# A two-layer hybrid decoder trunk: compression layer 1 in four column groups with its weights beside the ring, and sparse scores over 128 rows

## The reference, cut to what matters

```
h = RMSNorm(x); proj = h @ W_in            (columns shared out among four mixers and their gates)
o_A = NSA(compressed + selected + sliding window)     4 heads of 64
o_B = S5 state-space scan + GLU
o_C = gated DeltaNet, chunks of 64
o_D = stick-breaking attention
x = x + W_out( sum_m sigmoid(g_m(h)) * (o_m @ P_m) )
x = x + SwiGLU(RMSNorm(x))                 (hidden width 2816)
```

## Time and profile before

| | |
|---|---|
| time, median of 3 runs | 2307.31 us (2302.64 to 2307.64) |
| the profiled execution, its own time | 2303.84 us |
| its span in the trace | 2302.1 us |
| mean granted TensorE clock in it, share of full | 0.959 |
| TensorE matmul busy | 2120.3 us, 92% |
| VectorE, ScalarE, GpSimd busy | 1144.4, 758.9, 538.6 us |
| weight slabs loaded | 296 of 512 KB |

### The profile page before, as it was taken

One profiled execution on the slowest core, in us unless ns is written; L12 is line 12 of the kernel. 1 busy time (PEld: TensorE's weight loads), 2 busy tenths in 40 slices (PEclk: granted clock), 3 DMA queues, 4 the chain that ended last, 5 costly groups with the idle time before them and its releaser, 6 DMA issues.

```text
span 2302.1 us, 25818 instructions
## 1 busy us (share of the span) xinstructions
PE 2120.3 (92%) x10100; PEld 1676.2 (73%) x10100; DVE 1144.4 (50%) x1575; ACT 758.9 (33%) x1149; POOL 538.6 (23%) x300
## 2 busy tenths in 40 slices
PE   5989998899999899999988889888999998999998
PEld 3667976667677688888756679766566776888886
DVE  6344569763347544432273365796533475444321
ACT  5333231264334322222152332313642343222221
POOL 2336027523116000000032350374131250000000
PEclk9999999999989999999989999999989899999999
DMA  4232011222124223333233310123121342332332
GB/s 144 101 104 80 15 46 60 83 69 69 55 102 166 80 92 100 94 100 101 67 99 101 117 49 15 51 69 97 55 69 42 126 153 69 100 101 92 101 101 92
DMA packets 55124, 197.03 MB, mean 86 GB/s; under 512 B 6112, under 2 KB 6112, under 8 KB 52576
## 3 DMA queue, kind: packets, MB, share of 16 engines
q1 hardware_dynamic: 43488, 161.85, 22.1%
q10 hardware_dynamic: 11520, 33.56, 3.8%
HBM read 176.51 MB, written 18.87 MB: 85 GB/s over the span
## 4 chain that ended last, share of the span: by engine, by line
PE 36%; DVE 8%; POOL 2%; ACT 2%; DMA 1%; issue 1%; SPq 0%; POOLq 0%; DVEq 0%; PEldq 0%; ACTq 0%
PE bank L455 9%; PE bank L457 9%; PE bank L456 9%; DVE arena L1636 2%; DVE arena L1631 1%; DMA raw<-weights 1%; PE bank L904 1%; PE bank L662 1%; PE bank L865 1%; PE bank L642 1%; POOL wL L1859 1%; PE bank L792 1%; DVE wL L1320 1%; DVE arena L1802 1%; ACT wH L1005 0%
## 5 line engine op out<-in xcount | busy, mean ns | idle before, releaser
L455 PE MATMUL bank<-hH,wH 128*128 128x512 f32 (+1 forms) x1536 | 620.7, 404 | 54.9 <-POOL wL L1859 27.4
L456 PE MATMUL bank<-hL,wH 128*128 128x512 f32 (+1 forms) x1536 | 609.9, 397 | 0.0
L457 PE MATMUL bank<-hH,wL 128*128 128x512 f32 (+1 forms) x1536 | 608.4, 396 | 0.0
L1859 POOL TENSOR_TENSOR wL<-raw,wH 128x1024 fp32r<-128x1024 f32 x114 | 281.6, 2474 | 1232.7 <-ACT wH L1005 1232.5
L1005 ACT ACTIVATE wH<-raw 128x1024 fp32r<-128x1024 f32 x276 | 290.2, 1053 | 395.9 <-PE bank L457 231.7
L455 PEld LDWEIGHTS bank<-hH,wH 128*128 128x128 f32 (+1 forms) x1536 | 294.9, 192 | 135.3 <-issue 36.4
L457 PEld LDWEIGHTS bank<-hH,wL 128*128 128x128 f32 (+1 forms) x1536 | 293.6, 191 | 65.6 <-issue 1.0
L456 PEld LDWEIGHTS bank<-hL,wH 128*128 128x128 f32 (+1 forms) x1536 | 294.4, 192 | 61.8 <-issue 1.0
L1320 DVE TENSOR_TENSOR wL<-raw,wH 128x1024 fp32r<-128x1024 f32 x162 | 213.3, 1317 | 185.3 <-ACT wH L1005 185.2
L1008 ACT ACTIVATE gst<-bank 128x512 f32<-128x512 f32 x64 | 38.2, 596 | 351.1 <-PE bank L457 351.1
L457 PE MATMUL bank<-hidH,wL 128*128 128x512 f32 x352 | 140.4, 399 | 0.0
(11 more groups left out here) (380 smaller groups left out, 3008.1 us busy)
## 6 DMA issues: line engine op xcount, KB each, us to landing
raw<-weights SPq DMA_DIRECT2D x296, 512.0 KB, 3.5
gates<-gst ACTq DMA_DIRECT2D x64, 256.0 KB, 2.4
gload<-gates ACTq DMA_DIRECT2D x16, 1024.0 KB, 6.9
xT<-x SPq DMA_DIRECT2D x1, 2048.0 KB, 10.1
out<-xT SPq DMA_DIRECT2D x1, 2048.0 KB, 6.7
const<-constants SPq DMA_DIRECT2D x1, 1228.5 KB, 5.5
pack<-params SPq DMA_DIRECT2D x2, 451.0 KB, 3.9
cosT<-pos SPq DMA_DIRECT2D x1, 256.0 KB, 5.6
```

The lines of the kernel that those rows point to most:

```text
L455: mm(out, a[0], b[0], start=start, stop=False)
L456: mm(out, a[0], b[1], start=False, stop=False)
L457: return mm(out, a[1], b[0], start=False, stop=stop)
L1859: tt_(wL[:, ORD[i] % SPLIT], raw[:, i % RING], wH[:, ORD[i] % SPLIT].bitcast(F32), SU)\
```

## The change

1. The eight slabs of w1 leave the ring: `RAW` keeps only cw2 and glu, and a layer streams 140 slabs in place of 148. They lie behind the stream in the same array. ScalarE's own queue loads them at the start of the layer, four (v) after the third slab is split and four (k) after h is complete, into memory that is idle then (`arena`, `pj`, `sbv`), each set with a semaphore. TensorE waits for each set once and no longer waits for its own matmuls or releases a buffer there.
2. The blocks are padded from 31 to 32 columns (GpSimd clears the 32nd), and the four matmuls of a step write to partitions 0, 32, 64 and 96 onwards of the bank, each group adding up over the four steps. The four partial sums are added where the result was transposed: a matmul with the constant `stack` (128 x 31, four stacked identities) takes the place of each transpose.
3. The sparse scores take all 128 rows: the weights are both heads' queries (`nqr[:, h // 2, ...]`), the keys are `kpad[h % 2]`, which holds them in the half of that head and zeros in the other. VectorE clears the two halves (two memsets of 64 x 1024 after the third `nts`), and TensorE waits for that too.
4. The mask after the weights of stick-breaking is made from `ge` in one scalar_tensor_tensor, in place of an addition of `negk`, which leaves the constants. `abc_done` and `trig_done` count what `tab_ready` and `sin_ready` did.

```diff
-RAW = [f"ck{i}" for i in range(4)] + [f"cv{i}" for i in range(4)] + ["cw2", "glu"]
+RAW = ["cw2", "glu"]
...
-        bk = comp[:, 2, 0:496].rearrange("p (b n) -> p b n", b=16)
-        bv = comp[:, 3, 0:496].rearrange("p (b n) -> p b n", b=16)
+        bk = comp[:, 2, :].rearrange("p (b n) -> p b n", b=16)
+        bv = comp[:, 3, :].rearrange("p (b n) -> p b n", b=16)
...
+        cmp_w = [[x.rearrange("p (c n) -> p c n", c=4) for x in xs] for xs in (
+            [arena[:, 4096 + 1024 * j:5120 + 1024 * j] for j in range(4)],
+            [pj[:, TI["sb0"] + 2 * j:TI["sb0"] + 2 * j + 2, :].rearrange("p a s -> p (a s)") for j in range(2)]
+            + [sbv[:, :, :].rearrange("p t c -> p (t c)"), arena[:, 11264:12288]])]
...
-        nqn, nqr, nsq, nrs, kdup = tiles(0, 3), tiles(1536, 3), tiles(3072, 3), tiles(4608, 3), tiles(6144, 2)
+        nqn, nqr, nsq, nrs = tiles(0, 3), tiles(1536, 3), tiles(3072, 3), tiles(4608, 3)
+        kpad = (tiles(6144, 2), pj[:, 4:6, :])
...
-                            name = f"c{'kv'[kv]}{j}"
-                            w = raw_slab(name).rearrange("p (k c) -> p k c", k=4)
-                            for i in range(4 * j, 4 * j + 4):
-                                last = mm(PS[6 + kv][0:NCMP, 0:256], blocks[:, i, :], w[:, i % 4, :],
-                                          start=(i == 0), stop=(i == 15))
-                            raw_used(last, name)
+                            if j == 0:
+                                pe.wait_ge(cmp_loaded[kv], 64)
+                            for c in range(4):
+                                last = mm(PS[6 + kv][32 * c:32 * c + 32, 0:256], blocks[:, 4 * j + c, :], cmp_w[kv][j][:, c, :],
+                                          start=(j == 0), stop=(j == 3))
+                        last.then_inc(q["cmp_nat"], 1)
...
-                        last = nc.tensor.transpose(PS[5][:, 31 * c:31 * c + 31], cmpT[0:NCMP, P * c:P * c + P],
-                                                   ident[0:NCMP, 0:NCMP])
+                        last = mm(PS[5][:, 31 * c:31 * c + 31], cmpT[:, P * c:P * c + P], cst("stack")[:, 0:NCMP],
+                                  start=True, stop=True)
...
-                    pe.wait_ge(q["t_sin"], 3)
+                    pe.wait_ge(q["t_sin"], 4)
...
-                            mm(out[:, 0:wid], nqr[half(h), h // 2, P * qt:P * qt + P], kdup[half(h), br, 0:wid],
+                            mm(out[:, 0:wid], nqr[:, h // 2, P * qt:P * qt + P], kpad[h % 2][:, br, 0:wid],
...
                     high_to(SPLIT)
+                    for j in range(4):
+                        a.dma_start(cmp_w[1][j], a_w[layer, NSLAB + 4 + j].rearrange("p (c n) -> p c n", c=4))\
+                            .then_inc(cmp_loaded[1], 16)
+                    a.wait_ge(q["h_ready"], KT)
+                    for j in range(4):
+                        a.dma_start(cmp_w[0][j], a_w[layer, NSLAB + j].rearrange("p (c n) -> p c n", c=4))\
+                            .then_inc(cmp_loaded[0], 16)
...
-                        a.wait_ge(q["slab_done"], SLAB[f"c{'kv'[kv]}3"] + 1)
-                        act(cmpT[0:NCMP, 256 * kv:256 * kv + 256], PS[6 + kv][0:NCMP, 0:256], ACT.Copy)\
+                        a.wait_ge(q["cmp_nat"], kv + 1)
+                        act(cmpT[:, 256 * kv:256 * kv + 256], PS[6 + kv][:, 0:256], ACT.Copy)\
                             .then_inc(q["cmp_nat_ready"], 1)
-                    high_to(ahead(SLAB["cv3"]))
                     fill(FILL["hidden"])
...
-                    act(kdup[HD:P, 0, :], kdup[0:HD, 0, :], ACT.Copy).then_inc(q["kdup_ready"], 1)
-                    act(kdup[0:HD, 1, :], kdup[HD:P, 1, :], ACT.Copy).then_inc(q["kdup_ready"], 1)
+                    act(kpad[1][HD:P, 0, :], kpad[0][0:HD, 0, :], ACT.Copy).then_inc(q["kdup_ready"], 1)
+                    act(kpad[0][0:HD, 1, :], kpad[1][HD:P, 1, :], ACT.Copy).then_inc(q["kdup_ready"], 1)
...
-                        tt_(sb_z(h, kb)[:, c], sb_z(h, kb)[:, c], cst("negk"), A_).then_inc(q["d_masked"], 1)
+                        stt(sb_z(h, kb)[:, c], cst("ge"), NEG, sb_z(h, kb)[:, c], M, A_).then_inc(q["d_masked"], 1)
...
+                    v.memset(kpad[0][HD:P, :, :], 0.0)
+                    v.memset(kpad[1][0:HD, :, :], 0.0).then_inc(q["t_sin"], 1)
...
+                        g.memset(dst[:, :, NCMP:32], 0.0)
...
-                                tt_(kdup[r, x, :], nqr[r, i, :], nts[r, i, :], A_).then_inc(q["rot_ready"], 1)
+                                tt_(kpad[x][r, x, :], nqr[r, i, :], nts[r, i, :], A_).then_inc(q["rot_ready"], 1)
```

More of the change, by code:

```diff
@@ L82 @@
 SLAB = {}
-RAW = [f"ck{i}" for i in range(4)] + [f"cv{i}" for i in range(4)] + ["cw2", "glu"]
+RAW = ["cw2", "glu"]
 def _slabs():
     names = ["small"] + [n for n, _ in FIRST]
-    at = [sum(FILL["blocks"][:i + 1]) for i in range(8)] + [BEFORE_GELU + FILL["gelu"], GLU_AT]
+    at = [BEFORE_GELU + FILL["gelu"], GLU_AT]
     for i, n in enumerate(FILLERS):
@@ L124, in _const_columns @@
     for name, n in [("ident", P), ("ones", P), ("blk", P), ("le", P), ("ge", P), ("lt", P),
-                    ("negk", P), ("gt", P), ("lev", 7 * P), ("rot", P), ("freq", 1), ("cneg", NT * NCMP),
+                    ("gt", P), ("lev", 7 * P), ("rot", P), ("freq", 1), ("stack", 32), ("cneg", NT * NCMP),
                     ("c01", NT * NCMP), ("t", P), ("tc", 8 * NT)]:
@@ L277, in program @@
         gate_back = [sem(f"gate_back{i}") for i in range(4)]
+        cmp_loaded = [sem(f"cmp_loaded_{kv}") for kv in "kv"]
         q = {n: sem(n) for n in """
@@ L282, in program @@
             w_high sbv_half
-            blocks_ready cmp_nat cmp_nat_ready cmp_hid cmp1_ps  kc_ready
+            blocks_ready cmp_nat cmp_nat_ready cmp_hid cmp1_ps kc_ready
             sig_exp sig_ready xa_neg xa_ln g_ready gsum_ps gsum_taken gexp_ready
@@ L290, in program @@
             head_sq head_ss head_rstd z_tanh gdn_done
-            tab_ready sin_ready bu_ps m_ready w_ready z_ready n_ready x_ready y5_ps y5_ready y5_sq y5_tanh
+            bu_ps m_ready w_ready z_ready n_ready x_ready y5_ps y5_ready y5_sq y5_tanh
             gy_ready s5_done
@@ L1109, in _ @@
                     for kv in range(2):
-                        a.wait_ge(q["slab_done"], SLAB[f"c{'kv'[kv]}3"] + 1)
-                        act(cmpT[0:NCMP, 256 * kv:256 * kv + 256], PS[6 + kv][0:NCMP, 0:256], ACT.Copy)\
+                        a.wait_ge(q["cmp_nat"], kv + 1)
+                        act(cmpT[:, 256 * kv:256 * kv + 256], PS[6 + kv][:, 0:256], ACT.Copy)\
                             .then_inc(q["cmp_nat_ready"], 1)
-                    high_to(ahead(SLAB["cv3"]))
                     fill(FILL["hidden"])
-                    a.wait_ge(q["cmp_nat"], 1)
+                    a.wait_ge(q["cmp_nat"], 3)
                     act(cx, PS[5][:, 0:124], ACT.Copy).then_inc(q["cmp1_ps"], 1)
@@ L1168, in _ @@
                     fill(FILL["oss"])
-                    a.wait_ge(q["tab_ready"], 1)
-                    act(s5_sin, s5_sin, ACT.Sin, scale=SIN_SCALE).then_inc(q["sin_ready"], 1)
-                    act(s5_cos, s5_cos, ACT.Sin, scale=-SIN_SCALE, bias=TWO_PI / 4).then_inc(q["sin_ready"], 1)
+                    a.wait_ge(q["abc_done"], 3)
+                    act(s5_sin, s5_sin, ACT.Sin, scale=SIN_SCALE).then_inc(q["trig_done"], 1)
+                    act(s5_cos, s5_cos, ACT.Sin, scale=-SIN_SCALE, bias=TWO_PI / 4).then_inc(q["trig_done"], 1)
                     for i in range(8):
@@ L1589, in _ @@
                             turns(stage, *s5_turns)
-                    turns(6, *s5_turns).then_inc(q["tab_ready"], 1)
+                    turns(6, *s5_turns).then_inc(q["abc_done"], 1)
                     for i in range(2):
@@ L1619, in s5_turn_in @@
                         tt_(m4, s_, bur, M).then_inc(q["m_ready"], 1)
-                    v.wait_ge(q["sin_ready"], 2)
+                    v.wait_ge(q["trig_done"], 8)
                     s5_turn_in(0)
@@ L1869, in _ @@
                     for src, dst, pos in ((t2k, bk, prm("posk")), (t2v, bv, prm("posv"))):
+                        g.memset(dst[:, :, NCMP:32], 0.0)
                         for x in range(2):
                             view = src[:, 16 * x:16 * x + 496].rearrange("p (n b t) -> p b n t", b=8, t=2)[:, :, :, 0]
-                            tt_(dst[:, 8 * x:8 * x + 8, :], view,
+                            tt_(dst[:, 8 * x:8 * x + 8, 0:NCMP], view,
                                 pos[:, 8 * x:8 * x + 8].unsqueeze(2).broadcast_to([P, 8, NCMP]), A_)\
@@ L1968, in _stream @@
 def _stream(i, l):
-    out = np.zeros((NSLAB, P, KT * P), np.float32)
+    out = np.zeros((NSLAB + 8, P, KT * P), np.float32)
     def put(name, x):
@@ L1982, in _stream @@
     put("sbv1", v[:, 4:8])
-    for kv in "kv":
+    for n, kv in enumerate("kv"):
         w1 = i[f"nsa_cmp_{kv}_w1"][l].reshape(16, P, 256).transpose(1, 0, 2)
         for j in range(4):
-            put(f"c{kv}{j}", w1[:, 4 * j:4 * j + 4])
```

(3 more changed lines are left out.)

## The result

The changed kernel takes 2238.55 us (median of 4 runs, 2236.26 to 2240.88), the kernel before 2307.47 beside it: a ratio of 0.9705, 95% interval 0.9691 to 0.9718. The profiled execution took 2240.9, span 2239.1, so 63 us less than the profiled one before.

The account below looks back on a forecast made before the run. TensorE, busy for 92% of the span, was taken as the bound. Terms summed to 22.6 us per layer, 45 for two, giving 2259 from the profiled 2303.8 or 2262 from the median; predicted 2261, range 2243 to 2280.

Parts of the forecast that it names:

- The ring: Compression layer: without RAW slabs the split runs ahead and waits end; with the column groups, 11.3 us gained per layer.
- The column groups: Compression steps: four groups run at twice the pace of one, so a step costs 1.3 us in place of 2.92.
- that rival: Compression steps: four groups run at once, a step costs 0.7 us, 8 more gain, 2253; chance 0.08.
- The blocks: GpSimd's two added memsets on the path to step 0: 0.15 us each, a loss of 0.3 per layer.
- step 0: First compression step: gains nothing, as the tile behind it waits for a subtraction that GpSimd starts after the blocks.
- the stack: Sum of the partial results behind the last compression step: 1.0 us in place of 2.27, gain 1.3 per layer.
- the GELU: TensorE's 3.27 us wait for VectorE goes, gain 3.3; the low clock behind it mostly goes, gain 2.1.
- ScalarE's queue: Layer start: eight DMA instructions delay the first Exp by 3.4 us; 1.3 of it reaches TensorE, a loss.
- starved start: Layer start, rival: ring loads stand behind all eight new loads, 36 us lost in all, 2297; chance 0.06.
- The sparse scores: Sparse attention: fewer changes of array shape save 9.0 us of TensorE's time per layer, of which 6.2 stays.
- the clock stays up in the sparse part: Sparse attention, rival: with 128 rows at work the clock might not fall, 2 x 10 us more gain, 2241; chance 0.08.
- the two rivals that add to the gain: Four column groups run at once (2253, chance 0.08) and the clock stays up in the sparse part (2241, chance 0.08).

Follow-up runs that it names:

- ring_only: Changed kernel with all sixteen matmuls of a branch in one column group and the old transposes behind them; 2255.8 us, ratio 0.9783.
- two_0011: Changed kernel with two column groups in place of four, a step's four products going to groups 0, 0, 1, 1; 2246.7 us, ratio 0.9751.
- sc_only: Kernel before with only the sparse scores changed to 128 rows (zero-padded keys); 2287.2 us, ratio 0.9919.
- groups_in_ring: Kernel before with four column groups and the stacking matmuls, weights still in the ring's RAW slabs, old scores; 2300.3 us, ratio 0.9971.
- two_0101: Changed kernel with two column groups in place of four, a step's four products going to groups 0, 1, 0, 1; 2248.1 us, ratio 0.9751.
- mask64: Kernel before with each sparse score's mask matmul on the same 64 rows as the score; 2292.9 us, ratio 0.9941.
- half0: Kernel before with every sparse score and its mask matmul on rows 0 to 63, for both heads; 2308.0 us, ratio 0.9992.

## Why the prediction was wrong

- **The ring**: right. ring_only has no waits behind steps 1 to 7, and steps of 1.84, where the forecast had 2.0 for one group. Layer 2's steps before were 0.2 longer each than layer 1's (8.84 against 8.62), which counting one layer twice missed: 1.5 us.
- **The column groups**: this step failed. "Twice as fast is what in-order issue gives. ... That argument gives the same factor for four groups" was wrong: 0.57 per step and not 1.3, 14 x 0.73 = 10 us more. two_0011 shows that a waiting matmul doesn't hold up another group's. The row that the argument stood on had both signs in it: two groups at twice the pace fit either law, and I took the one with a story. The Trainium skill ("TensorE: Matmul & The Clock Gate", Part 3) had this outcome, and the trace agrees in the main: 0.57 for four tiles of two records each. The starts are 7 ns apart, where the page has some 4. I gave that rival 0.08 because no row had more than two groups; that absence spoke for neither side.
- **The blocks, step 0, the stack and the GELU**: right. The blocks take 0.09 us longer (forecast 0.3). Step 0 gained nothing (the wait behind it grew by 1.27, as its matmuls shrank). L558 costs 0.81 against 2.27 before, a gain of 1.5 (forecast 1.3). The GELU's wait and the low clock behind it are gone; but 3 us in layer 1 and 1.6 in layer 2 were given back in the recurrences, with phases of low clock that moved.
- **ScalarE's queue**: the size (1.8 and 0.9 us against 1.3) came out right by luck. By the forecast's own mechanism 0.2 reached TensorE in layer 1: VectorE's short operation gave 2.1 back, as forecast, but the issues delayed the Exp by 2.3 and not by 3.4. The rest came by the granted clock, which I hadn't counted there and which stayed full in two other kernels with the same start. The "starved start" did not occur. The ring's loads have a median of 3.5 us as before; the one that goes out at 38.39, among the new ones, took until 45.49, ScalarE waited 1.31 us for it, and TensorE didn't wait.
- **The sparse scores**: 6.2 per layer were forecast, 8 and 13 came. As TensorE's own time it was too much, since VectorE's wait took 4.6 of it in both layers (forecast 3.4). Of the 7.3 and 13.7 us that the stretch gains in sc_only, 20 - 13 = 7 and 38 - 13 = 25 us less at the low level make, at half speed and over 90% busy, about 3.5 and 11.5. By this estimate about 4 and 2 us are the scores' own. What I had as the rival "the clock stays up in the sparse part" (0.08) happened in part, and mostly in layer 2, whose windows I hadn't read.
- **The sum**: in the profiled executions 45 us were forecast and 63 came. Of the 18 missed, 10 are the groups, 1.5 layer 2's steps and some 9 the sparse stretch (21 for 12.4), less the 4.6 given back in the recurrences, which the forecast didn't have: 16 in all. The other 4 of the 22 between 2261 and 2238.5 are no effect of the change: the forecast was set 2 us above its own sum from the profiled execution, and the changed kernel's profiled execution was 2.3 above the median. The range excluded the result because it took each of the two rivals that add to the gain as an end by itself. The one happened in full and the other in part, together.

Still open: why the clock in before's layer 1 fell for only 20 us and for 38 in the five other stretches with scores on 64 rows and masks on 128. The same instructions begin there behind a different history, and no run varied that alone.

## What to carry to other kernels

Small float32 matmuls in different column groups of the array ran fully side by side here, and with two groups in both orders tried, so count the longest group and not the sum; but first look at what paces them: inside the ring the same edit gained 6 us with all that came with it, outside it the groups alone gave 17 of 69. In this kernel a matmul on half the rows cost twice, once in its own time where its neighbours use all rows, and once in the clock; padding with zeros to 128 rows can be the faster form. And read the granted clock in each layer: the same code had 0.91 in one and 0.84 in the other.

## What the runs showed of the hardware

- Float32 matmuls of 256 columns in one, two and four column groups: four of them take 1.84, 1.0 and 0.57 us (ring_only, two_0101, the changed kernel), with two groups in either order (two_0011).
- Scores on 64 rows in different halves run two at a time, too, when no matmul on 128 rows stands between them (mask64: 4.5 us busy for 9.0).
- With only rows 0 to 63 at work in 96 of the 535 records of a stretch that was 93% busy, the granted clock was 0.79 and 0.87 (half0, in its slowest execution of ten); with 128 rows it was 0.94 at 91% busy (sc_only). With the scores alone on 64 rows, and not side by side, it was 0.84 in five stretches of six.
- Where waits of 2 to 4 us stood between column tiles, the clock was 0.89 over 60 us (groups_in_ring, in its slowest execution of ten); with waits of 0.3 to 1.4 in the same tiles before, it was 1.00.
